# Ring loads issued first, the scaled input transposed a second time, and S5's kernel in one bank

## The chip, the cores and the metric

One core of a Trainium2 chip runs the whole program in one launch. The metric is the device time in microseconds (us) of one execution; the median of several is given. The engines are TensorE (PE in the rows; PEld is its weight load), VectorE (DVE), ScalarE (ACT), GpSimd (POOL) and SyncE (SP); each works through its own instructions in order and waits on semaphores for the others. SP issues the weight loads, ACT and POOL issue a few DMAs as well.

## What is computed

The reference is three layers over a sequence of 256 tokens with 1024 features, each with a modulation of its normed input by a condition vector. What matters here is the first step of the first layer and one constant matrix of the third:

```python
def ada_modulate(x, c, norm_g, ada_w, ada_b):
    ada = jax.nn.silu(c) @ ada_w + ada_b
    shift, scale, gate = jnp.split(ada, 3, axis=-1)
    h = rmsnorm(x, norm_g) * (1.0 + scale[:, None, :]) + shift[:, None, :]
    return h, gate[:, None, :]

def s5_mixer(u, lambda_re, lambda_im, log_dt, b_re, b_im, c_re, c_im, d_skip, glu_w, glu_b):
    ...
    lam_bar = jnp.exp(lam * dt)
    b_bar = ((lam_bar - 1) / lam)[..., None] * b
    bu = jnp.einsum('gpc,bsgc->bsgp', b_bar, uf.astype(jnp.complex64))
    _, states = lax.associative_scan(_ssm_combine, (a, bu), axis=1)
    y = jnp.einsum('gcp,bsgp->bsgc', c, states).real \
        + d_skip.astype(jnp.float32).reshape(SSM_GROUPS, SSM_GROUP_CH) * uf
```

## The kernel before, in words

**Weights and products.** All weights are f32 in HBM and stream through `ring`, ten slots of 128x1024 (512 KB each), loaded by SP in the order of `unit_list`. A unit is two slots ("halves"). A slot of a product's weights is rounded by ACT to fp32r (`WH`, in `cut` at L1088, four buffers), DVE subtracts to get the rest (`WL`, L1530, four buffers), and PE makes three matmuls per tile: high times high, high times low, low times high (`mm3`, all recorded at L554). A slot of modulation weights ("ada", 16 halves for the first two thirds, shift and scale, of the first layer) is not multiplied on PE as a rule: DVE adds slot times silu(c) into `ACC` (chunk 0, shift) or `ACC2` (chunk 1, scale, in `SQT`), L1543 for a chunk's first half and L1546 for the others; PE then sums over the partitions with `ones` (`ada_sum`, 8 matmuls). The halves in `ADA_PE` go to PE instead (`ada_half`). An f32 matmul leaves two records in the trace, an fp32r one or a transpose one.

**The start.** The ten ring slots begin to be loaded behind nine small loads of vectors (`packs[0]`) on SP. PE transposes the vectors (`vc0`), x as it is (`xt0` to `xt3`, 16 transposes, copied to `xT` by ACT), does halves 1 and 3 by `ada_half`, spreads the rsqrt of the mean squares over the partitions (`r0`), does `vc1`, half 6, the sum of chunk 0, half 11, half 14 and the sum of chunk 1, with `warm` matmuls (of the identity, their result unused) in between. DVE makes the other halves, then the low parts of two weight slots (`cut(1 - AHEAD_L)`), then both additions of the bias, `GS` = (1 + scale) times gain, and `modulate`: for each of eight blocks of 128 features, SQT = xT * GS * r (L1626), then ACT rounds SQT + shift to `hh`, then DVE makes `hl` (L1631). The first product, `v0`, is 48 matmuls of 256 columns and begins when block 0 is there. `M0` holds the modulation's result, `SIL` the silu(c).

**S5's kernel.** In the third layer the matrices `TOEP` are made beside the first feed-forward (`ffn`), by generators that advance one step for each half unit (`side.run`). `s5_weights` makes 16 products of `BK` (128 x 32) with `CL` (128 x 128), real and imaginary part added up, so 32 f32 matmuls: four groups `tp0` to `tp3` of eight, each in a bank of its own taken from the rotation (`open_`), partitions 0 to 31, with one step between them. ACT copies each group into four diagonal blocks of TOEP, four copies per group and one group per step. DVE adds `ssm_d` to the diagonal afterwards (`s5_skip`). There are four rotating PSUM banks, `pw`; a bank opened with `hold` comes back into the rotation by `back` only.

## Time and profile before

| | us |
|---|---|
| median of 3 runs | 1041.58 |
| lowest, highest | 1039.48, 1042.46 |
| the profiled execution, device time | 1039.8 |
| its span in the trace | 1038.1 |
| TensorE busy | 999.2 (96%) |
| VectorE busy | 720.7 (69%) |
| ScalarE busy | 507.7 (49%) |
| mean granted TensorE clock | 0.995 of full |

The profiled execution is 1.8 us below the median. Its device time is 1.7 us more than its span. TensorE is busy nearly throughout, so that a microsecond counts where TensorE waits, runs at a lower clock, or has fewer instructions to do. The DMA engines are busy 95% or more over most of the first 50 us and 40 to 75% afterwards.

### The profile page before, as it was taken

What the parts mean: (1) busy time and instruction counts of PE and PEld (TensorE: products, weight loads), DVE (VectorE), ACT (ScalarE), POOL (GpSimd) and SP (SyncE); (2) the same over time, 40 slices, a digit from 0 to 9 for tenths busy, and PEclk for the clock granted to TensorE, in tenths of its full rate; (3) what the DMA queues carried; (4) which work ended last, traced back from release to release, by engine and by line L of the source; (5) the groups of instructions that cost most, each with busy time, mean ns of one, the idle gap of its engine ahead of it and who ended that gap; (6) DMA issues with size and microseconds to landing.
All of it is one profiled execution on the core that took longest, in us unless ns stands there. A gap on an engine that the chain in (4) does not pass through costs nothing.

```text
span 1038.1 us, 19534 instructions
## 1 busy us (share of the span) xinstructions
PE 999.2 (96%) x8198; PEld 987.0 (95%) x8198; DVE 720.7 (69%) x1021; ACT 507.7 (49%) x741; POOL 41.0 (4%) x67
## 2 busy tenths in 40 slices
PE   6999999999999999999999999999997999999998
PEld 5899999999999999999999999998997999999998
DVE  4767876777746845667999788678877666465554
ACT  2554354456544454634754564555465454444442
POOL 2100000000000013401000000000000000000000
PEclk9999999999999999999999999999998999999999
DMA  9987486656764976469477667664433446466621
GB/s 355 366 279 244 163 284 244 218 189 229 258 203 134 315 242 214 155 245 298 152 247 263 233 244 247 240 236 153 160 103 105 139 154 208 166 227 195 212 98 42
DMA packets 138960, 219.58 MB, mean 212 GB/s; under 512 B 7161, under 2 KB 110922, under 8 KB 138872
## 3 DMA queue, kind: packets, MB, share of 16 engines
q1 hardware_dynamic: 136776, 214.00, 59.9%
q10 hardware_dynamic: 1136, 2.58, 0.7%
q0 software_dynamic: 960, 1.76, 0.6%
q8 instruction: 65, 1.06, 0.4%
q14 instruction: 23, 0.19, 0.1%
HBM read 217.25 MB, written 1.05 MB: 210 GB/s over the span
## 4 chain that ended last, share of the span: by engine, by line
PE 86%; DVE 7%; issue 2%; ACT 2%; DMA 2%; SPq 0%; ACTq 0%; DVEq 0%
PE pw L554 63%; PE pacc L554 22%; DVE WL L1530 2%; DMA ring<-in_even_in_w 1%; ACT AR L1088 1%; DVE hl L1631 1%; DVE SQT L1626 1%; DVE ACC L1546 1%; DMA AR<-in_cond 0%; ACT hh L1088 0%; ACT WH L1088 0%; PE pw L935 0%; PE pw L722 0%; SPq L311 0%; ACT YH L1088 0%
## 5 line engine op out<-in xcount | busy, mean ns | idle before, releaser
L1088 ACT ACTIVATE WH<-ring 128x1024 fp32r<-128x1024 f32 x288 | 302.0, 1055 | 268.8 <-PE pw L554 190.8
L554 PE MATMUL pw<-hh,WH 128*128 128x256 f32 x1408 | 404.2, 287 | 8.3 <-DVE WL L1530 4.3
L1530 DVE TENSOR_TENSOR WL<-ring,WH 128x1024 fp32r<-128x1024 f32 x288 | 344.3, 1223 | 81.5 <-ACT WH L1088 81.0
L554 PE MATMUL pw<-hl,WH 128*128 128x256 f32 x1408 | 399.0, 283 | 0.0
L554 PE MATMUL pw<-hh,WL 128*128 128x256 f32 x1408 | 399.0, 283 | 0.0
L554 PEld LDWEIGHTS pw<-hh,WH 128*128 128x128 f32 x1408 | 270.4, 192 | 12.1 <-issue 9.9
L554 PEld LDWEIGHTS pw<-hl,WH 128*128 128x128 f32 x1408 | 270.5, 192 | 0.0
L554 PEld LDWEIGHTS pw<-hh,WL 128*128 128x128 f32 x1408 | 270.4, 192 | 0.0
L554 PE MATMUL pacc<-YH,WH 128*128 128x256 f32 x672 | 192.6, 287 | 3.5 <-issue 2.5
L554 PE MATMUL pacc<-YH,WL 128*128 128x256 f32 x672 | 191.0, 284 | 0.0
L554 PE MATMUL pacc<-YL,WH 128*128 128x256 f32 x672 | 191.0, 284 | 0.0
L1088 ACT ACTIVATE AR<-pw 128x512 f32<-128x512 f32 (+5 forms) x196 | 86.2, 453 | 129.4 <-PE pw L554 128.5
L554 PEld LDWEIGHTS pacc<-YH,WH 128*128 128x128 f32 x672 | 129.6, 193 | 4.4 <-issue 4.4
L554 PEld LDWEIGHTS pacc<-YL,WH 128*128 128x128 f32 x672 | 129.7, 193 | 0.0
L554 PEld LDWEIGHTS pacc<-YH,WL 128*128 128x128 f32 x672 | 129.7, 193 | 0.0
L1546 DVE SCALAR_TENSOR_TENSOR ACC<-ring,PC,ACC 128x1024 f32<-128x1024 f32 x95 | 122.0, 1284 | 7.7 <-DMA ring<-in_ada_w 2.0
L554 PE MATMUL pw<-WH,hh 128*128 128x256 f32 x192 | 55.4, 289 | 2.3 <-DVE hl L1631 2.2
L2035 DVE TENSOR_TENSOR AR<-AR,pw 128x256 f32<-128x256 f32 x44 | 16.5, 418 | 58.9 <-ACT AR L1088 58.9
L1575 DVE TENSOR_TENSOR YL<-AR,YH 128x512 fp32r<-128x512 f32 x48 | 32.8, 691 | 34.7 <-ACT YH L1088 34.5
L554 PE MATMUL pw<-AR 128*128 128x128 f32 (+6 forms) x416 | 55.9, 287 | 0.9 <-ACT AR L1088 0.9
L554 PE MATMUL pw<-WH,hl 128*128 128x256 f32 x192 | 55.2, 287 | 0.0
L554 PE MATMUL pw<-WL,hh 128*128 128x256 f32 x192 | 55.1, 287 | 0.0
(245 smaller groups left out, 853.4 us busy)
## 6 DMA issues: line engine op xcount, KB each, us to landing
ring<-in_w_mod SPq DMA_DIRECT2D x72, 512.0 KB, 5.8
ring<-in_odd_in_w SPq DMA_DIRECT2D x56, 512.0 KB, 6.9
ring<-in_ada_w SPq DMA_DIRECT2D x48, 512.0 KB, 8.0
ring<-in_ffn_w_gate SPq DMA_DIRECT2D x44, 512.0 KB, 5.0
ring<-in_ffn_w_up SPq DMA_DIRECT2D x44, 512.0 KB, 5.3
ring<-in_ffn_w_down SPq DMA_DIRECT2D x44, 512.0 KB, 4.8
ring<-in_even_in_w SPq DMA_DIRECT2D x40, 512.0 KB, 6.8
ring<-in_even_out_w SPq DMA_DIRECT2D x16, 512.0 KB, 5.8
```

What stands on the lines that cost most here:

```text
L554: return eng.matmul(o, a, b, start=start, stop=stop, skip_group_check=True)
L1088: return eng.activation(dst, src, func, **kw)
L1530: tt(WL[:, i % NL, :], slot(half_of(i)), WH[:, i % NH, :].bitcast(F32), SUB).then_inc(s_lo, 1)
L1546: stt(out=acc, in0=slot(g), scalar=wc, in1=acc, op0=MUL, op1=ADD).then_inc(s_ada, 1)
L1575: tt(f2(YL[:, i % 3]), src, f2(YH[:, i % 3]).bitcast(F32), SUB).then_inc(s_yl, 1)
L1626: stt(out=SQT[:, k, :], in0=xT[:, k, :], scalar=GS[:, k:k + 1], in1=rb, op0=MUL, op1=MUL).then_inc(s_u, 1)
L1631: stt(out=hl[:, q, :], in0=SQT[:, q, :], scalar=m[:, q:q + 1], in1=hh[:, q, :].bitcast(F32), op0=ADD, op1=SUB).then_inc(s_hl, 1)
L2035: tt(fbuf(blk, m), fbuf(blk, m), pw[b][:, T:2 * T], MUL).then_inc(s_bank[b], 1)
```

## The change

- **Queues at the start.** SP issues nothing but ring loads. `packs[0]` now holds only `c` and `cond` and goes first on ACT's queue, then the identity, then x; the other seven vectors (`packs[1]`) and the rest of `consts` are issued by ACT after the two Exp. POOL has the last two packs, and its later loads wait for ring load 19 where they waited for 15.
- **Order of the modulation.** The scale half of the weights is loaded first (chunk 0 is now the scale, chunk 1 the shift). PE takes halves 1, 3, 6, 9 and 12.
- **x times r.** ACT multiplies XN by the rsqrt (two passes of 128x1024 into `XR`), PE transposes that too (`xr0` to `xr3`, 16 transposes), ACT copies it to SQT and multiplies it by GS. The spread `r0` and the L1626 pass of DVE are gone for the first layer. The shift is summed and added in two halves (`ada1a`, `ada1`), and hh and hl of blocks 0 to 3 follow the first. One weight slot is cut ahead of them where three (ACT) and two (DVE) were.
- **S5's kernel.** One bank `tp`, held: the matmul of index m writes partitions 32m to 32m+31, index q the columns. 32 matmuls in one step, m innermost, seven steps later the bank returns. ACT's 16 copies stay four to a step.

```diff
-ADA_PE = (1, 3, 6, 11, 14)
+ADA_PE = (1, 3, 6, 9, 12)
...
-    units += ada(a0, 0, 2)
+    units += ada(a0, 1, 2) + ada(a0, 0, 1)
...
-    for key, ms in (("p0", (0, 2, 4)), ("p1", (5, 7, 8, 9, 10)), ("p2", (12, 13)), ("p3", (15,))):
+    for key, ms in (("p0", (0, 2, 4)), ("p1", (5, 7)), ("p2", (8, 10)), ("p3", (11,)), ("p4", (13, 14, 15))):
...
             p.wait_ge(d_vec[0], n_vec[0])
             pb = open_("vc0")
             close(eng.transpose(pb[:, 0:n0], VR[0:n0, 0, :], ident[0:n0, 0:n0]), "vc0")
...
             ada_half(1)
             ada_half(3)
+            p.wait_ge(d_x, 16)
+            turn(XN, "xt")
...
+            close(last, "vc1")
+            ada_half(6)
+            p.wait_ge(s_xr, 2)
+            turn(XR, "xr")
+            p.wait_ge(*ada_done(7))
...
-            close(eng.transpose(pb[:, n1:n1 + n2], VR[0:n2, 2, :], ident[0:n2, 0:n2]), "vc1")
-            ada_half(6)
-            ada_sum(0)
-            ada_half(11)
+            ada_sum(0, range(8), "ada0")
...
+            p.wait_ge(*gone["ada0"])
+            ada_half(9)
+            ada_half(12)
+            warm(8, "warm0a")
+            p.wait_ge(*ada_done(15))
+            ada_sum(1, range(4), "ada1a")
+            ada_sum(1, range(4, 8), "ada1")
+            warm(8, "warm0c")
...
                 for q in range(4):
-                    pb = open_(f"tp{q}")
-                    for m in range(4):
-                        for i in range(2):
-                            last = mm(pb[0:32, m * P:m * P + P], BK[i][:, 4 * q + m, :], CL[i][:, 4 * q + m, 0:P],
-                                      m == 0 and i == 0, i == 1)
-                    close(last, f"tp{q}")
-                    yield
+                    for i in range(2):
+                        for m in range(4):
+                            last = mm(pb[32 * m:32 * m + 32, q * P:q * P + P], BK[i][:, 4 * q + m, :],
+                                      CL[i][:, 4 * q + m, 0:P], q == 0 and i == 0, i == 1)
+                close(last, "tp")
+                yield from idle(7)
+                back("tp")
...
+            s.wait_ge(s_r, 1)
+            for m in range(2):
+                act(XR[:, m, :], XN[:, m, :], scale=RS[:, m:m + 1]).then_inc(s_xr, 1)
+            for q in range(4):
+                evac(f"xr{q}", SQT[:, 2 * q:2 * q + 2, :], src=v3(pw[place[f"xr{q}"]][:, :], 2))
             evac("dt", DTC, src=pw[place["dt"]][:, 0:16], func=ACT.Exp)
+            s.wait_ge(s_gs, 1)
+            for k in range(8):
+                s.wait_ge(*gone[f"xr{k // 2}"])
+                act(SQT[:, k, :], SQT[:, k, :], scale=GS[:, k:k + 1]).then_inc(s_u, 1)
...
-            pack_loads(eng.dma_start, 1, d_vec[1])
             pack_loads(eng.dma_start, 2, d_vec[2])
...
-            g.wait_ge(*landed(15))
+            g.wait_ge(*landed(19))
```

How the order of the engines moves, at three places. TensorE, from the first layer's last modulation halves to the first product (`pacc<-PC,ring` is `ada_half`, `pacc<-cst,ACC` or `SQT` or `AR` a sum of a chunk, `pw<-cst` a warm, `pw<-WH,hh` the first product's first matmul); the kernel before:

```order
L554 MATMUL pacc<-PC,ring 128x128 [waits s_ring1]
L554 MATMUL pacc<-PC,ring 128x128 x7
L740 MATMUL pw0<-cst,AR 128x16 [waits s_lam,s_bank0]
L554 MATMUL pw1<-cst 128x128 [waits s_fill]
L554 MATMUL pw1<-cst 128x128 x7
L554 MATMUL pacc<-PC,ring 128x128 [waits s_ring4]
L554 MATMUL pacc<-PC,ring 128x128 x7
L554 MATMUL pw3<-cst 128x128 [waits s_bank3]
L554 MATMUL pw3<-cst 128x128 x3
L554 MATMUL pacc<-cst,SQT 128x128 [waits s_ada]
L554 MATMUL pacc<-cst,SQT 128x128 x7
```

and the changed one, from its sum of the scale chunk on:

```order
L557 MATMUL pacc<-cst,ACC 128x128 [waits d_cst,s_ada]
L557 MATMUL pacc<-cst,ACC 128x128 x7
L750 MATMUL pw2<-cst,AR 128x16 [waits s_lam,s_bank2]
L557 MATMUL pacc<-PC,ring 128x128 [waits s_ring9,s_mod]
L557 MATMUL pacc<-PC,ring 128x128 x7
L557 MATMUL pacc<-PC,ring 128x128 [waits s_ring2]
L557 MATMUL pacc<-PC,ring 128x128 x7
L557 MATMUL pw3<-cst 128x128 [waits s_bank3]
L557 MATMUL pw3<-cst 128x128 x7
L557 MATMUL pacc<-cst,AR 128x128 [waits s_ada]
L557 MATMUL pacc<-cst,AR 128x128 x7
```

Halves 9 and 12 now stand behind the addition of the scale (`s_mod`), and nothing but one warm stands between them and the last sum.

VectorE, from the last modulation half to the first hl; the kernel before:

```order
L1546 SCALAR_TENSOR_TENSOR SQT<-ring,PC,SQT 128x1024 [waits s_ada,s_ring5]
L1530 TENSOR_TENSOR WL<-ring,WH 128x1024 [waits s_hi] x2
L1551 TENSOR_TENSOR MOD<-pacc,VC 128x8 [waits s_fill]
L1551 TENSOR_TENSOR MOD<-pacc,VC 128x8
L1615 SCALAR_TENSOR_TENSOR PC<-MOD,VC 128x8 [waits s_mod]
L1626 SCALAR_TENSOR_TENSOR SQT<-xT,PC,pw2 128x256 [waits s_v]
L1626 SCALAR_TENSOR_TENSOR SQT<-xT,PC,pw2 128x256
L1631 SCALAR_TENSOR_TENSOR hl<-SQT,MOD,hh 128x256 [waits s_hh]
```

and the changed one, from half 10 on:

```order
L1574 SCALAR_TENSOR_TENSOR AR<-ring,PC,AR 128x1024 [waits s_ada,s_ring0]
L1672 TENSOR_TENSOR MOD<-pacc,VC 128x8 [waits s_fill,s_bank1]
L1704 SCALAR_TENSOR_TENSOR PC<-MOD,VC 128x8 [waits s_mod]
L1574 SCALAR_TENSOR_TENSOR AR<-ring,PC,AR 128x1024 [waits s_ada,s_ring1]
L1708 TENSOR_TENSOR RS<-VC,PC 128x16 [waits s_bank2]
L1574 SCALAR_TENSOR_TENSOR AR<-ring,PC,AR 128x1024 [waits s_ada,s_ring3]
L1574 SCALAR_TENSOR_TENSOR AR<-ring,PC,AR 128x1024 [waits s_ada,s_ring4]
L1574 SCALAR_TENSOR_TENSOR AR<-ring,PC,AR 128x1024 [waits s_ada,s_ring5]
L1672 TENSOR_TENSOR MOD<-pacc,VC 128x4 [waits s_fill]
L1558 TENSOR_TENSOR WL<-ring,WH 128x1024 [waits s_hi]
L1678 SCALAR_TENSOR_TENSOR hl<-SQT,MOD,hh 128x256 [waits s_hh,s_u,s_mod]
```

The scale's addition stands ahead of four halves; behind the last half one low part (L1558) is left where two were, and no L1626.

TensorE at the first group of S5's kernel (`32x128`), the kernel before and the changed one:

```order
L554 MATMUL pw2<-hh,WL 128x256
L554 MATMUL pw3<-AR 32x128 [waits s_bank3,s_cl,s_bk]
L554 MATMUL pw3<-AR 32x128 x7
L554 MATMUL pw0<-hh,WH 128x256 [waits s_lo]
L554 MATMUL pw0<-hl,WH 128x256
```

```order
L557 MATMUL pw0<-hh,WL 128x256
L557 MATMUL pw2<-AR 32x128 [waits s_bank2,s_cl,s_bk]
L557 MATMUL pw2<-AR 32x128 x31
L557 MATMUL pw3<-hh,WH 128x256 [waits s_lo]
L557 MATMUL pw3<-hl,WH 128x256
```

All 32 stand in one place, ahead of the last quarter of a feed-forward block.

## Rows read from the trace of the kernel before

**Rows 1.** The page's busy times: us, share of the span, instructions.
```profile
PE 999.2 (96%) x8198; PEld 987.0 (95%) x8198; DVE 720.7 (69%) x1021; ACT 507.7 (49%) x741; POOL 41.0 (4%) x67
```
**Rows 2.** What TensorE waited for, whole span: us in total, times, longest.
```profile
PE pw L716 <- DMA AR<-in_cond: 9.2, 1, 9.2
PE pw L554 <- DVE hl L1631: 5.0, 5, 2.2
```
**Rows 3.** The chain of waits, first 45 us: start us, us, what.
```profile
21.74 10.95 DMA ring<-in_even_in_w
...
33.80 1.23 DVE WL L1530
```
**Rows 4.** Timeline, 20 to 45 us: start, us, engine, line, what [idle before].
```profile
29.70 1.28 DVE L1546 SCALAR_TENSOR_TENSOR SQT<-ring,PC,SQT 128x1024 f32<-128x1024 f32 x1 [1.28 <-DMA ring<-in_ada_w]
...
31.11 1.97 PE L554 MATMUL pacc<-cst,SQT 128*128 128x128 f32 x16
31.21 1.06 ACT L1088 ACTIVATE WH<-ring 128x1024 fp32r<-128x1024 f32 x1 [2.54 <-DMA ring<-in_even_in_w]
...
34.21 1.06 ACT L1088 ACTIVATE WH<-ring 128x1024 fp32r<-128x1024 f32 x1 [0.45 <-DMA ring<-in_even_in_w]
34.94 0.23 DVE L1551 TENSOR_TENSOR MOD<-pacc,VC 128x8 f32<-128x8 f32 x2
...
36.47 0.49 DVE L1631 SCALAR_TENSOR_TENSOR hl<-SQT,MOD,hh 128x256 fp32r<-128x256 f32 x1 [0.18 <-ACT hh L1088]
...
37.10 0.36 PE L554 MATMUL pw<-WH,hh 128*128 128x256 f32 x1 [2.22 <-DVE hl L1631]
...
41.84 1.28 ACT L1157 ACT_TABLE_LOAD   x1
```
**Rows 5.** Stretches: us, busy (records) of each engine, PEclk, DMA share, GB/s.
```profile
0.00:9.00 9.00, 0.00 (x0) 0.00 (x0) 0.00 (x0) 1.28 (x1) 6.87 (x17) 1.00 0.76 254
4.00:9.00 5.00, 0.00 (x0) 0.00 (x0) 0.00 (x0) 0.00 (x0) 4.01 (x9) 1.00 1.04 361
9.00:25.00 16.00, 14.83 (x107) 14.46 (x108) 11.89 (x26) 4.32 (x10) 0.00 (x0) 1.00 1.03 410
37.00:42.00 5.00, 4.90 (x28) 4.93 (x29) 4.82 (x13) 3.21 (x7) 0.00 (x0) 0.66 1.06 350
```
**Rows 6.** Timeline, first 20 us: start, us, engine, line, what [idle before].
```profile
4.37 15.37 SPq L2295 DMA_DIRECT2D ring<-in_ada_w  x16
9.17 0.43 PE L716 MATMUL pw<-cst,AR 116*128 116x116 f32 x1 [9.17 <-DMA AR<-in_cond]
...
9.39 3.62 PE L722 MATMUL pw<-cst,AR 128*128 128x128 f32 x16
...
11.07 0.75 DVE L1543 TENSOR_SCALAR ACC<-ring,PC 128x1024 f32<-128x1024 f32 x1
...
12.81 4.42 PE L554 MATMUL pacc<-PC,ring 128*128 128x128 f32 x32
15.09 1.28 DVE L1546 SCALAR_TENSOR_TENSOR ACC<-ring,PC,ACC 128x1024 f32<-128x1024 f32 x1 [1.23 <-DMA ring<-in_ada_w]
```
**Rows 7.** Timeline, end of the program: its 16 output transposes.
```profile
1031.26 1.91 PE L1075 MATMUL pw<-cst,AR 128*128 128x128 f32 x16
```
**Rows 8.** Timeline around S5's groups `tp0` and `tp1`, ScalarE and TensorE.
```profile
669.77 1.78 ACT L1088 ACTIVATE AR<-pw 32x128 f32<-32x128 f32 x4 [0.87 <-PE pw L554]
...
672.46 0.28 PE L554 MATMUL pw<-hh,WL 128*128 128x256 f32 x1
672.67 1.93 PE L554 MATMUL pw<-AR 128*32 128x128 f32 x16
674.53 0.39 PE L554 MATMUL pacc<-YH,WH 128*128 128x256 f32 x1
674.76 0.28 PE L554 MATMUL pacc<-YL,WH 128*128 128x256 f32 x1
674.88 0.28 PE L554 MATMUL pacc<-YH,WL 128*128 128x256 f32 x1
```

More of the change, by code:

```diff
@@ L339, in build @@
         d_id, d_cst, d_x = sem("d_id"), sem("d_cst"), sem("d_x")
-        d_vec = [sem(f"d_vec{a}") for a in range(3)]
-        n_vec = [16 * len(packs[0]), 16 * len(packs[1]), 16 * (len(packs[2]) + 1)]
+        d_vec = [sem(f"d_vec{a}") for a in range(4)]
+        n_vec = [16 * len(pk) for pk in packs[:3]] + [16 * (len(packs[3]) + 1)]
         d_sguw, d_sgub, d_glr, d_glw = sem("d_sguw"), sem("d_sgub"), sem("d_glr"), sem("d_glw")
@@ L351, in build @@
         s_silu = sem("s_silu")
+        s_xr = sem("s_xr")
+        s_gs = sem("s_gs")
         s_x2 = sem("s_x2")
@@ L420, in build @@
         fg = col("final_g", 0, 8)
-        ACC2 = f2(SQT[:, 0:4, :])
+        ACC2 = ar(14720, 1024)
         GT = v3(ar(0, 4096), 16)
@@ L513, in ysc @@
             return last
-        full, gone, place = {}, {"ada0": (s_mod, 1), "ada1": (s_mod, 2)}, {}
+        full, gone, place = {}, {"ada0": (s_mod, 1), "ada1": (s_mod, 3)}, {}
         block = ctx.enter_context(nc.Block())
@@ L693, in norm_mod @@
                 back(f"r{L}")
-            n0, n1, n2 = pack_n
+            n0, n1, n2, n3 = pack_n
             def ada_half(m):
@@ L703, in ada_half, with ada_sum @@
                     last = mm(pacc[:, j, c * P:c * P + P], slot(g)[:, j * P:j * P + P],
-                              SIL[:, m % 8:m % 8 + 1].to_broadcast([P, P]), m in (1, 11) and j % 2 == 0, False)
+                              SIL[:, m % 8:m % 8 + 1].to_broadcast([P, P]), m == 1 and j % 2 == 0, False)
                 last.then_inc(s_adp, 1)
-            def ada_sum(c):
-                p.wait_ge(*ada_done(8 * c + 7))
-                for j in range(8):
+            def ada_sum(c, js, name):
+                for j in js:
                     last = mm(pacc[:, j, c * P:c * P + P], (ACC, ACC2)[c][:, j * P:j * P + P], ones, False, True)
-                close(last, f"ada{c}")
+                close(last, name)
             p.wait_ge(d_id, 16)
@@ L740, in _ @@
             close(eng.transpose(pb[:, 0:16], DTR, ident[0:16, 0:16]), "dt")
-            warm(8, "warm0b")
-            ada_half(14)
-            warm(4, "warm0c")
-            ada_sum(1)
-            warm(8, "warm0d")
-            back("r0")
+            p.wait_ge(*gone["ada0"])
[6 more added lines that the diff above has]
+            warm(8, "warm0c")
             for j in range(4):
@@ L1125, in yhigh, with modulate @@
                 act(f2(YH[:, i % 3]), src).then_inc(s_yh, 1)
-            def modulate(L, sh):
-                for k in range(8):
+            def modulate(L, sh, ks=range(8)):
+                for k in ks:
                     s.wait_ge(s_u, 8 * L + k + 1)
@@ L1387, in s5_prep @@
                 s.wait_ge(s_tz, 7)
-                for q in range(4):
-                    b = place[f"tp{q}"]
-                    pb = pw[b][:, :].rearrange("p (a t n) -> p a t n", a=4, t=4)
-                    s.wait_ge(*full[f"tp{q}"])
+                b = place["tp"]
+                pb = v3(pw[b][:, :], 4)
+                s.wait_ge(*full["tp"])
+                for m in range(4):
                     for blk in range(4):
-                        r = slice(32 * blk, 32 * blk + 32)
-                        to = TOEP[r, 4 * q:4 * q + 4, 32 * (3 - blk):].rearrange("p a (t n) -> p a t n", n=32)
-                        last = act(to, pb[0:32, :, 0:blk + 1, :])
-                        if blk < 3:
+                        last = act(TOEP[32 * blk:32 * blk + 32, m:16:4, 32 * (3 - blk):],
+                                   pb[32 * m:32 * m + 32, :, 0:32 * blk + 32])
+                        if m < 3 or blk < 3:
                             last.then_inc(s_tp, 1)
@@ L1548, in ada @@
                     elif what == "add":
[L1549 to L1553 removed]
+                        v.wait_ge(*full[f"ada{c}"])
                         b = place[f"ada{c}"]
@@ L1642, in update, with first_add, first_lows @@
                 v.wait_ge(s_x, X_FIN[L] + 8)
-            n0, n1, n2 = pack_n
+            def first_add(c, to, j0, n, name):
+                v.wait_ge(*full[name])
+                tt(MOD[:, to:to + n].unsqueeze(2), pacc[:, j0:j0 + n, c * P:c * P + 1],
+                   col("ada_b", to, n).unsqueeze(2), ADD).then_inc(s_mod, 1)
+            def first_lows(ks):
+                for k in ks:
+                    v.wait_ge(s_hh, k + 1)
+                    stt(out=hl[:, k, :], in0=SQT[:, k, :], scalar=M0[:, k:k + 1], in1=hh[:, k, :].bitcast(F32),
+                        op0=ADD, op1=SUB).then_inc(s_hl, 1)
+            n0, n1, n2, n3 = pack_n
             v.wait_ge(*full["vc0"])
@@ L2017, in s5_skip @@
                 yield from idle(6)
-                v.wait_ge(s_tp, 12)
-                for q in range(4):
-                    v.wait_ge(*gone[f"tp{q}"])
+                v.wait_ge(s_tp, 15)
+                v.wait_ge(*gone["tp"])
                 for b in range(4):
```

89 lines of the change are left out of this document (52 added, 37 removed).

## The prediction

> **What bounds the kernel now.** I read the busy times first: TensorE is busy 96% of the span [rows 1]. The list of what TensorE waited for comes next: 9.2 us at the very start, for `cond` to land, and 5.0 us in five waits for hl, of which the longest, 2.2, stands before the first product [rows 2]. From the first product on, at 37.10, TensorE has nearly no gap for 100 us. So the program is a start of 37.10 us and then TensorE's own work; a start that is earlier by a microsecond should end the program a microsecond earlier.
>
> What bounds the start? The chain of waits goes through DMA for 10.95 us from 21.74 [rows 3]. The timeline agrees: VectorE waited 1.23 us for modulation half 4 (used at 15.09) and 1.28 us for half 15 (used at 29.70) [rows 4, 6]. Eleven slots in 14.61 us are 1.33 us each, which is what 512 KB take at the 410 GB/s of that stretch [rows 5]. Behind half 15 stand VectorE's pass (1.28), the sum (31.11 to 33.1), but then no addition until 34.94: VectorE was still on a low part, 33.80 to 35.03 [rows 3, 4]. Addition, GS, SQT, hh and hl take the 2.1 us to 37.10. TensorE idled 2.2 us there, and over 37 to 42 its mean granted clock is 0.66 of full: it fell to the lower level, 1.2 GHz, after that pause [rows 4, 5].
>
> **DMA from the first moment.** In the first 9 us the queues moved 254 x 9 = 2.29 MB [rows 5]. The ring's first load was issued at 4.37 [rows 6]. If the ring is issued at 0.8 and data flows from about 2.3 us, 6.7 us at 361 to 410 GB/s are 2.42 to 2.75 MB: 0.3 to 1.1 us of loading ahead. I take 0.9, near the rate of the long stretch, because 4 KB rows of weights will then flow beside the small ones. Half 15 lands at 28.8, its pass ends at 30.1. The landing of c, cond and identity costs nothing: before, silu was ready at 11.07 [rows 6], and the first slot is not there before 7.5 or 8.
>
> **The scaled transposes.** They put a new chain on the start: half 4 (14.1), VectorE's pass and rsqrt (to 17.2), two ACT passes of 1.06 behind the copies of xt (to 20.4), 16 transposes, the sum of the scale, VectorE's addition, and only behind that halves 11 and 13 to 15. The transposes cost 1.9 us at full clock [rows 7] and 3.6 at the lower one [rows 6]; the trace shows that level for the first 16 and the higher one within the 32 records behind them. Where TensorE stands at each step: half 1 from 8.9 and half 3 from 12.8 (they wait for their slots), xt to 17.5, half 6 to 19.9, xr to 22.3, sum to 24.2. VectorE has finished half 10 at 23.2, waits 1.1 us for the sum, does the addition, GS and half 11 to 26.0, and half 13 lands at 26.1. So the new wait is just covered, with next to nothing to spare; every microsecond that it is later shows. Queued behind that addition on TensorE is half 9, and behind half 9's slot all of SP's later loads (piece 3 of the first product and on). Half 9 ends at 26.6, while the load before stands in the queue until 33: covered.
>
> **From half 15 to the first product.** Half 9 and 12 and a warm fill TensorE to 30.5. Half a sum is 1.0 us (half of 1.97, rows 4): the first half-addition is at 31.8. ACT's WH0 is made by then (31.21 + 1.06 less 0.9). hh0 to 32.4, low part 0 on VectorE 31.9 to 33.1, hl0 to 33.65. TensorE has the other half sum and a warm (2.0) until 34.4, so it begins at 34.4: **2.7 us earlier**, and without a pause. A mean of 0.66 over 5 us is 3.4 us at half the clock; 256 columns take 0.213 us at 1.2 GHz and 0.12 per record otherwise [rows 8], so 16 records took 0.093 longer each: **1.5 us** to gain if the clock holds. Against it: ACT has cut one slot ahead instead of three. It does hh0 to hh3, WH1, hh4 to hh7 (to 37.1), the table load of 1.28 [rows 4], then WH2 (to 39.5); low part 2 is ready at 40.7, and TensorE, 48 x 0.12 = 5.8 us after 34.4, wants it at 40.2: **0.5 lost**. The start gives 2.7 + 1.5 - 0.5 = 3.7. The piece that was last to be late there is WH3 (its slot is free once half 9 is done), wanted 3 us later.
>
> POOL's loads (1.1 MB for the spatial gate) now wait for ring load 19, 5 us later; the transposes that use them stand behind four products, 23 us after the start: nothing. SP loses nine issues. DVE loses eight passes and ACT gains fourteen (XR, the copies of xr, the multiplication by GS), the last of them between the scale's addition at 24.5 and WH0 at 30.2, 5.7 us for eight passes of about 0.5 (as hl, rows 4): covered.
>
> **S5's kernel.** A group of eight costs TensorE, from the matmul before (672.46) to the first after (674.53), 2.07, less the 0.12 that a matmul takes anyway, plus 0.11 by which the one after is longer (674.76 - 674.53 against 0.12): 2.06 us, 1.86 for 16 records and 0.2 for going in and out [rows 8]. Four groups: 8.2 us, all on the path, for TensorE has no gap there. In one group the 0.2 is paid once: 0.6 saved for sure. What 32 matmuls cost whose outputs lie in four different strips of partitions no row shows. They may run one after the other (0.6 saved), or four at a time: 64 x 0.116 / 4 = 1.9 + 0.2, 6.2 saved. I take two at a time, 3.7 + 0.2 = 3.9, **4.3 saved**, the middle: that the array's columns are free for it speaks for four, that every record of this trace, of 64, 128 or 256 columns, takes 0.11 to 0.12 us speaks for a cost per instruction that overlap doesn't remove. ACT's copies stay as they were (1.78 per step); the first waits for all 32, up to 675.4 instead of 669.8, while ACT has nothing due before the feed-forward's own copy, which stands behind TensorE's last 24 matmuls: covered. One bank less for seven steps leaves three; a block holds two, a modulation sum one, and a block's banks are copied out during the 5.8 us of the down projection: covered.
>
> The Trainium skill (TensorE: Matmul & The Clock Gate, Part 3: Packing small matmuls) has outputs in different 32-partition strips run concurrently, three of them measured 2.38 times as fast; by that the 7.4 us would be 3.1 and the sum 0.6 us better. No row here shows it.
>
> **Sum.** 3.7 + 4.3 = 8.0. The profiled execution of 1039.8 becomes 1031.8. It lies 1.8 below the median; what is compared are medians, so 1041.58 - 8.0 = **1033.6**.
>
> **Rivals.**
> 1. *The strips don't overlap.* 3.7 + 0.6 = 4.3, **1037.3**. For it: 0.11 to 0.12 us per record everywhere. Against: only 128-column weights were ever loaded at that rate.
> 2. *They overlap fully.* 3.7 + 6.2 = 9.9, **1031.7**.
> 3. *TensorE is at the lower clock during the second transposes.* The first 16 ran at 3.6 us, and the clock rose only within the halves behind them [rows 6]. Now TensorE's first 10 us are broken by waits for slots and followed by 32 transposes. If xr and the sum run at 1.2 GHz, they cost 1.6 + 1.5 more, with no cover: the start gives 0.6, in all 4.9 with the strips overlapped by two (**1036.7**), 1.2 without (1040.4). Against: the output transposes ran at full clock, but straight behind matmuls [rows 7]. The Trainium skill (TensorE: Matmul & The Clock Gate, Part 4: PE-mode transpose) says that transposes don't count as TensorE activity for the clock; rows 6 fit that and fit a plain delay as well.
> 4. *The ring overtakes what the start needs; slower.* Ring, c, cond, identity and x are now issued at the same moment. If c and cond were served behind the ten slots, 5.2 MB at 410 GB/s, they would land at 15 instead of 9. VectorE's eleven halves, rsqrt and copies are 15.6 us of work from there: half 15 done at 32.9, the scale chain adds 1, TensorE begins at 38.2. That is 1.1 later, with pause and clock as before, plus the 0.5 for low part 2, less 0.6 if the strips don't overlap: **1042.6**. It decides from a landing at about 14 us on. Against: `cond` landed 5.05 us after issue amid the same traffic.
>
> **Chances.** Forecast 0.38, rival 2 0.10, rival 1 0.26, rival 3 0.22, rival 4 0.04. The range of eight in ten goes from rival 2 less a microsecond of scatter, 1030.5, to rival 3's middle, 1039.5. A measurement of this kernel can tell about 0.3%, 3.1 us, from nothing. Faster by more: forecast and rival 2, most of rival 1 (4.3) and half of 3: 0.78. Within: 0.18. Slower: 0.04.
>
> **What would show it.** First product's first matmul at 34 to 35 us, with the clock at 1.00 in the 5 us behind it; VectorE idle about 1 us before the scale's addition; a wait of TensorE for WL of about 0.5 us near 40; one block of 64 records with `128*32` weights, about 3.7 us long (7.4 and 1.9 are rivals 1 and 2). A first matmul after 36, or xr at 3.4 us, is rival 3; silu after 14 is rival 4. I would be wrong altogether if the time won at the start were given back at a later wait; behind the first product DMA has slack (the share of its engines' time falls, see the table), so I don't expect that.

## The result, and the profile after

| | before | after |
|---|---|---|
| median, us (4 runs each, taken together) | 1041.21 | 1033.49 |
| lowest, highest | 1039.48, 1042.46 | 1031.64, 1034.32 |
| the profiled execution, device time | 1039.8 | 1033.03 |
| its span in the trace | 1038.1 | 1031.0 |
| TensorE busy | 999.2 | 992.2 |
| mean granted TensorE clock in it | 0.995 | 0.993 |

The ratio is 0.9925, 95% interval 0.9904 to 0.9945: 7.7 us less, where 8.0 were forecast. The sum came out; two of its terms did not, and their errors cancel, which is luck.

I read the timeline of the start first. TensorE of the changed kernel (start, length, engine and line, shapes, count; in brackets the idle time before and what ended it; L557 is before's L554):

```profile
7.43 0.28 PE L719 MATMUL pw<-cst,AR 16*128 16x16 f32 x1 [7.43 <-DMA cst<-in_consts]
9.09 5.30 PE L557 MATMUL pacc<-PC,ring 128*128 128x128 f32 x32 [1.38 <-DVE PC L1688]
14.23 1.91 PE L729 MATMUL pw<-cst,AR 128*128 128x128 f32 x16
...
19.05 1.97 PE L729 MATMUL pw<-cst,AR 128*128 128x128 f32 x16 [0.55 <-ACT AR L1101]
20.85 1.95 PE L557 MATMUL pacc<-cst,ACC 128*128 128x128 f32 x16
...
30.74 2.05 PE L557 MATMUL pacc<-cst,AR 128*128 128x128 f32 x16 [1.98 <-DVE AR L1574]
32.62 1.95 PE L557 MATMUL pw<-cst 128*128 128x128 f32 x16
34.33 0.36 PE L557 MATMUL pw<-WH,hh 128*128 128x256 f32 x1
...
40.40 0.36 PE L557 MATMUL pw<-WH,hh 128*128 128x256 f32 x1
```

Against [rows 4, 6]: both sets of 16 transposes take 1.9 us, where the first set took 3.62; the first product begins at 34.33 instead of 37.10; the second product's first matmul is at 40.40, 6.07 us behind it. VectorE over the same stretch:

```profile
21.51 1.28 DVE L1574 SCALAR_TENSOR_TENSOR AR<-ring,PC,AR 128x1024 f32<-128x1024 f32 x1 [1.22 <-DMA ring<-in_ada_w]
22.91 0.17 DVE L1672 TENSOR_TENSOR MOD<-pacc,VC 128x8 f32<-128x8 f32 x1
...
26.62 4.06 DVE L1574 SCALAR_TENSOR_TENSOR AR<-ring,PC,AR 128x1024 f32<-128x1024 f32 x3 [2.06 <-DMA ring<-in_ada_w]
31.93 0.16 DVE L1672 TENSOR_TENSOR MOD<-pacc,VC 128x4 f32<-128x4 f32 x1 [1.25 <-PE pacc L557]
32.01 1.21 DVE L1558 TENSOR_TENSOR WL<-ring,WH 128x1024 fp32r<-128x1024 f32 x1
33.14 1.66 DVE L1678 SCALAR_TENSOR_TENSOR hl<-SQT,MOD,hh 128x256 fp32r<-128x256 f32 x4
```

VectorE never waits for the scale's sum; it waits for slots, 1.2 and 2.1 us. Half 13 is there at 26.62. Then S5's kernel, TensorE's block with the matmul around it, and VectorE behind it:

```profile
664.75 0.28 PE L557 MATMUL pw<-hh,WL 128*128 128x256 f32 x1
664.96 1.96 PE L557 MATMUL pw<-AR 128*32 128x128 f32 x64
666.84 0.39 PE L557 MATMUL pw<-hh,WH 128*128 128x256 f32 x1
...
676.57 0.36 PE L557 MATMUL pw<-hh,WH 128*128 128x256 f32 x1 [0.82 <-DVE WL L1558]
```
```profile
670.50 0.75 DVE L2081 TENSOR_TENSOR AR<-AR,pw 128x256 f32<-128x256 f32 x2 [5.92 <-ACT AR L1101]
672.01 0.69 DVE L1599 TENSOR_TENSOR YL<-AR,YH 128x512 fp32r<-128x512 f32 x1 [0.76 <-ACT YH L1101]
672.62 2.66 DVE L1574 SCALAR_TENSOR_TENSOR ACC<-ring,PC,ACC 128x1024 f32<-128x1024 f32 x2
675.20 4.85 DVE L1558 TENSOR_TENSOR WL<-ring,WH 128x1024 fp32r<-128x1024 f32 x4
```

All 64 records in the time that 16 took [rows 8], and a new wait of 0.82 us for a low part ten microseconds later. Last, the clock, in stretches (PE, PEld, DVE, ACT and POOL busy, then PEclk, the granted clock; DMA share, GB/s), the changed kernel:

```profile
0.00:9.00 9.00, 0.28 (x1) 0.18 (x1) 0.81 (x5) 1.59 (x3) 6.87 (x17) 1.00 0.80 299
...
30.00:36.00 6.00, 5.26 (x46) 5.26 (x47) 4.75 (x10) 4.80 (x9) 0.50 (x1) 1.00 1.07 372
36.00:42.00 6.00, 5.93 (x50) 5.75 (x49) 4.59 (x8) 5.97 (x8) 2.35 (x4) 1.00 1.09 360
135.00:140.00 5.00, 3.23 (x21) 3.05 (x21) 4.90 (x6) 3.56 (x7) 0.00 (x0) 0.85 0.52 152
140.00:145.00 5.00, 5.00 (x36) 5.00 (x36) 2.38 (x3) 2.62 (x5) 0.00 (x0) 0.81 0.99 326
...
780.00:785.00 5.00, 3.64 (x18) 3.45 (x18) 4.41 (x13) 1.67 (x3) 0.00 (x0) 0.52 0.55 179
785.00:790.00 5.00, 3.48 (x22) 3.29 (x21) 1.96 (x8) 1.93 (x5) 0.00 (x0) 0.80 0.36 111
790.00:795.00 5.00, 4.01 (x23) 4.04 (x24) 4.62 (x9) 3.16 (x7) 0.00 (x0) 0.66 0.01 3
```

and the kernel before at the same pause of TensorE (1.8 us, at 140 there, at 136 after), with no fall:

```profile
140.00:145.00 5.00, 3.20 (x25) 2.83 (x24) 4.90 (x7) 3.37 (x7) 0.00 (x0) 1.00 0.67 204
```

The 1.00 of the first stretch says little: [rows 5] have it over 9 to 25 us too, though the 16 transposes at 9.39 took 3.62 us [rows 6], about twice the 1.91 of [rows 7]. The fall behind the first product's start is gone, one at 138 us has come, and the stretch around 780 to 795 is slower. Where the time went is seen best by landmarks. For every ScalarE record that two traces share in order, I took the difference of their starts, and the median of these around a point. Negative is earlier than the changed kernel, whose own times stand at the head:

| near (us, after) | 60 to 139 | 145 to 400 | 645 | 688 to 775 | 800 to the end |
|---|---|---|---|---|---|
| before | 3.96 | 2.76 | 2.78 | 7.87 | 7.08 |
| start_only | 0.34 | 0.56 | 2.05 | 7.13 | 4.96 |
| tp_only | 4.03 | 4.03 | 5.69 | 5.70 | 3.5 |
| tp_in_turn | 0.35 | -0.86 | -0.84 | 3.16 | 1.42 |
| tp_pairs | 0.12 | 0.14 | 1.85 | 3.19 | 2.34 |
| pe14 | 0.06 | 0.26 | 1.76 | 1.76 | 0.28 |
| ring_behind | 1.76 | 0.56 | 0.78 | 0.78 | -0.68 |
| tp_shift | 1.64 | 0.46 | 0.51 | 2.32 | 1.48 |
| fill_pause | 0.28 | -0.92 | -0.52 | -0.52 | -2.23 |
| no_warm0c | 0.35 | -0.86 | -0.10 | -0.10 | -2.28 |
| table_later | 0.11 | -1.10 | -0.32 | -0.31 | -1.80 |
| best | 0.21 | -1.00 | 0.53 | 0.53 | -2.08 |

Before minus after: 4.0 gained at the start (2.77 by the earlier first product, about 1.6 by the clock behind it, less the wait of 0.35 at 40), 1.2 lost at 138 us, 5.1 gained at S5's kernel (2.78 to 7.87), 0.8 lost around 780. Steps of 1.2 to 1.5 at 138 and 640, and of up to 2.2 around 780 to 800, come and go between kernels that are equal there. They go with falls of the clock, and the last experiments are about these. Steps of 0.2 to 0.9 between 400 and 500 us (ring_first, fill_pause, no_warm0c, table_later) have no fall beside them; their cause stays open.

### The profile page after: what moved, and what is told of

Its sections match the earlier page's. It is cut to its first block, busy times and chain, and to the rows that moved or that the text cites. A ratio compares the mean times of both kernels' runs of the same rounds, so it can differ in the third digit from the quotient of the medians.

```text
span 1031.0 us, 19531 instructions
## 1 busy us (share of the span) xinstructions
PE 992.2 (96%) x8191; PEld 980.8 (95%) x8191; DVE 717.1 (70%) x1014; ACT 514.4 (50%) x755; POOL 41.0 (4%) x67
## 3 DMA queue, kind: packets, MB, share of 16 engines
q0 software_dynamic: 960, 1.76, 0.6%
## 4 chain that ended last, share of the span: by engine, by line
PE 85%; DVE 8%; issue 3%; ACT 2%; DMA 2%; ACTq 0%; DVEq 0%
PE pw L557 63%; PE pacc L557 22%; DVE WL L1558 2%; DMA ring<-in_ada_w 1%; ACT AR L1101 1%; DVE ACC L1574 1%; DVE hl L1655 1%; DVE SQT L1650 1%; DMA cst<-in_consts 1%; DVE AR L1574 0%; ACT hh L1101 0%; PE pw L947 0%; ACT YH L1101 0%; DVE AR L2081 0%; ACT WH L1101 0%
## 5 line engine op out<-in xcount | busy, mean ns | idle before, releaser
L557 PE MATMUL pw<-hh,WH 128*128 128x256 f32 x1408 | 403.3, 286 | 9.1 <-DVE WL L1558 5.1
L1558 DVE TENSOR_TENSOR WL<-ring,WH 128x1024 fp32r<-128x1024 f32 x288 | 343.9, 1222 | 79.7 <-ACT WH L1101 76.4
L557 PE MATMUL pw<-hh,WL 128*128 128x256 f32 x1408 | 398.3, 283 | 0.0
L557 PE MATMUL pw<-hl,WH 128*128 128x256 f32 x1408 | 398.3, 283 | 0.0
L557 PEld LDWEIGHTS pw<-hh,WH 128*128 128x128 f32 x1408 | 269.9, 192 | 12.8 <-issue 10.7
L557 PEld LDWEIGHTS pw<-hl,WH 128*128 128x128 f32 x1408 | 270.0, 192 | 0.0
L557 PEld LDWEIGHTS pw<-hh,WL 128*128 128x128 f32 x1408 | 269.9, 192 | 0.0
L557 PE MATMUL pacc<-YH,WH 128*128 128x256 f32 x672 | 192.1, 286 | 3.5 <-issue 2.5
L557 PE MATMUL pacc<-YH,WL 128*128 128x256 f32 x672 | 190.6, 284 | 0.0
L557 PE MATMUL pacc<-YL,WH 128*128 128x256 f32 x672 | 190.6, 284 | 0.0
L557 PEld LDWEIGHTS pacc<-YH,WH 128*128 128x128 f32 x672 | 129.6, 193 | 4.0 <-issue 4.0
L557 PEld LDWEIGHTS pacc<-YL,WH 128*128 128x128 f32 x672 | 129.6, 193 | 0.0
L557 PEld LDWEIGHTS pacc<-YH,WL 128*128 128x128 f32 x672 | 129.4, 193 | 0.0
L557 PE MATMUL pw<-WH,hh 128*128 128x256 f32 x192 | 54.7, 285 | 0.2
L557 PE MATMUL pw<-WL,hh 128*128 128x256 f32 x192 | 54.3, 283 | 0.0
L557 PE MATMUL pw<-WH,hl 128*128 128x256 f32 x192 | 54.3, 283 | 0.0
L557 PE MATMUL pw<-AR 128*128 128x128 f32 (+6 forms) x416 | 50.1, 287 | 0.9 <-ACT AR L1101 0.9
```

Of the source, the lines that this page charges most:

```text
L557: return eng.matmul(o, a, b, start=start, stop=stop, skip_group_check=True)
L1558: tt(WL[:, i % NL, :], slot(half_of(i)), WH[:, i % NH, :].bitcast(F32), SUB).then_inc(s_lo, 1)
```

## The experiments

**One part alone.** `start_only` is the changed kernel with S5's kernel in four banks as before; `tp_only` is the kernel before with the new block.

> The changed kernel with S5's kernel as before (four groups in four banks). If the parts add up, the start alone gives what the changed kernel's trace shows at its second product, 4.0 us, less what the clock takes back. The changed trace has a fall of the clock at 138 us, behind a pause of TensorE of 1.8 us that the kernel before has as well (at 140) without a fall. Theory P (the fall depends on where the pause lies in time, and the start moves it there): the same fall here at 138, 1.2 us lost, first matmul of the S5 groups 2.8 us earlier than before (667.74), in all 2.8 us better than before, about 1038.4 if before is 1041.2. Rival Q (the change's data traffic or bank order behind the start causes it): no fixed place, other falls. Rival R (the start's gain survives in full): 4.0 better, 1037.2, no fall at 138. The new wait of 0.8 us for WL behind the S5 block (676.6 in the changed trace) is absent.

> The kernel before with S5's kernel in one bank, nothing else. The block of 64 records lasts 1.96 us as in the changed kernel; the path is 6.2 us shorter at its end, of which about 1.1 goes back by a wait for WL that comes some 9 us later, since TensorE comes sooner than VectorE can: net 5.1, about 1036.1 if before is 1041.2. If that wait were an effect of the start instead, net would be 6.2 (1035.0). No fall of the clock near 140 (as before), one at 38 us.

Measured, in 12 and 6 runs: start_only 1037.71, ratio 0.9962 (0.9947 to 0.9976), 3.5 us less than before's 1041.22; tp_only 1036.41, ratio 0.9944 (0.9923 to 0.9965), 4.8 less. Together 8.3, and both at once 7.7: within their intervals the parts add up. In tp_only TensorE waited 0.8 us once for WL between 660 and 702 us, in start_only and before never: the new wait belongs to the S5 block, not to the start. Theory P got no support, though: tp_only has the start of before, with the same pause at the same time (140.4), and its clock fell behind it, at 143 us, where I expected no fall. So the place of the pause in time doesn't decide it.

**How the strips overlap.** `tp_in_turn` finishes one strip before the next; `tp_pairs` alternates between two strips.

```diff
-                for q in range(4):
-                    for i in range(2):
-                        for m in range(4):
+                for m in range(4):
+                    for q in range(4):
+                        for i in range(2):
```
```diff
-                for q in range(4):
-                    for i in range(2):
-                        for m in range(4):
+                for m0 in (0, 2):
+                    for q in range(4):
+                        for i in range(2):
+                            for m in (m0, m0 + 1):
```

> The changed kernel with the same 32 matmuls into the same bank and strips, but all eight of a strip before the next strip (m is the outer loop). If it is the overlap of neighbours in different strips that makes the block 1.96 us long, it is now about 64 x 0.116 = 7.4 us plus 0.2. If it were the single entry and exit, or a lower cost of these matmuls in a strip layout as such, it stays near 2.

> The changed kernel with the 32 matmuls of S5's kernel ordered so that only strips 0 and 1 alternate in the first 16 and strips 2 and 3 in the last 16 (the changed kernel goes round all four strips; a run with one strip after the other took 5.96 us for the 64 records, the changed one 1.96). If what counts is how many different strips are under way at once, this takes about twice 1.96, 3.5 to 4.1 us. If overlap comes from neighbouring instructions that merely differ in strip, it takes 2.0 to 2.4.

The block in tp_in_turn and, below it, in tp_pairs (timeline of TensorE, with the wait that follows):

```profile
664.12 5.96 PE L557 MATMUL pw<-AR 128*32 128x128 f32 x64
679.73 0.36 PE L557 MATMUL pw<-hh,WH 128*128 128x256 f32 x1 [0.82 <-DVE WL L1558]
```
```profile
666.81 3.29 PE L557 MATMUL pw<-AR 128*32 128x128 f32 x64
679.75 0.36 PE L557 MATMUL pw<-hh,WH 128*128 128x256 f32 x1 [0.83 <-DVE WL L1559]
```

5.96, 3.29 and 1.96 us for one, two and four strips under way: 1.8 and 3.0 times as fast. It is the round over the strips that makes the overlap, not the single bank; 3.29 is a little under the 3.5 to 4.1 that I expected by the number of strips, and well above the 2.0 to 2.4 of the other reading. The Trainium skill (TensorE: Matmul & The Clock Gate, Part 3: Packing small matmuls) gives 2.38 for three strips, measured with 512 columns; with 128 columns no run here has three, and 2.38 lies between the two and the four strips above. My 7.6 us for the one strip was too much: 0.093 us a record, not 0.116.

The two runs answer a second question. The 0.82 us wait is the same in all three though the block is 0, 1.3 and 4.0 us longer. So it is not that VectorE fell behind a TensorE that had saved more. Behind the block ScalarE copies out the down projection (670.08 in the changed kernel, 673.25 and 673.26 in the other two), and from there VectorE needs two additions, YL, two modulation halves and one WL, so that TensorE starts 6.48 to 6.49 us after that copy in all three. Before, TensorE did another group of eight (1.93 us) in this stretch [rows 8]; pulling the groups together took that cover away. Net savings by the landmarks (645 to 688 us) are 1.09, 3.75 and 5.09 us in turn, in pairs and in fours; gross ones (8.24, four groups of 2.06, less the block and its 0.13 of going in and out) are 2.15, 4.82 and 6.15. So 1.06 to 1.07 us is given back each time, 0.82 of it in that wait.

**The block elsewhere.** `tp_shift` moves it three steps back (idle 22, 18 and 9 for 19, 15 and 6 on TensorE, ScalarE and VectorE).

> The changed kernel with the whole S5 block three steps later on TensorE, ACT and VectorE, so that it stands half a feed-forward block away. Theory: of the 6.2 us that the block saves TensorE, 0.8 to 1.1 are given back at 676 to 688 us, where VectorE, which stood still until 670.5 for the down projection's result, has two modulation halves and then the low parts to make; three steps later VectorE has no such pause behind the block and TensorE waits less there: landmarks at 700 us 0.5 to 1 earlier than in the changed kernel against the same point before the block. Rival: VectorE and ACT set the pace in this stretch wherever the block stands (they are 6 us behind once TensorE is 6 us faster), and the same 0.8 to 1.1 us are lost within the next 30 us.

The theory's expectation fell, and so did the rival's size. The wait near 677 went, but a larger one came (timeline of TensorE, tp_shift):

```profile
695.76 0.36 PE L557 MATMUL pacc<-YH,WH 128*128 128x256 f32 x1 [2.23 <-DVE WL L1558]
```

The landmarks stand at +0.5 before the block and +2.3 behind it: 1.8 us less saved than in the changed kernel. So moving the block did not bring back what the wait costs; at the new place VectorE was further behind.

**DMA at the start.** `ring_first` is the kernel before with its nine small loads on ACT's queue, so that the ring goes out at once; `ring_behind` is the changed kernel with seven of these loads ahead of the ring on SP.

```diff
+            pack_loads(eng.dma_start, 0, d_vec[0])
             eng.dma_start(cst[:, 0:P], I["consts"][:, 0:P]).then_inc(d_id, 16)
...
-            pack_loads(eng.dma_start, 0, d_vec[0])
             piece_at = {half_of(n): n for n in range(NPIECE)}
```

> The kernel before with its nine small vector loads issued by ScalarE ahead of the identity and x, so that SP begins with the ring loads at 0.8 us instead of 4.4. Theory D (the start was bound by loading, and loading ahead is worth what the first 9 us carry more): half 15 lands 0.3 to 1.1 us earlier, first product at 36.0 to 36.8 instead of 37.10. Rival S (x, now issued at 4.5 us and behind ring loads, comes late): x lands after 13 us, TensorE does its transposes before halves 1 and 3 and all slots come free later; first product at 37.5 to 39, slower by 0.5 to 2.

> The changed kernel with the seven other vectors' loads issued by SP ahead of the ring again, as in the kernel before, instead of by ACT behind the Exp; so the ring's first load is issued about 3 us later, all else as changed. It tells what the early issue of the ring alone is worth. Theory: little, since in the changed kernel half 13 landed only 0.4 us before its time in the kernel before (26.6 against 27.05) though the ring was issued 3.5 us earlier: half 13 lands at 26.9 to 27.2, the first product at 34.6 to 34.9. Rival: the queue's lead is worth its full time and something else (x, c, identity in the same queues) ate it: half 13 lands at 28 or later and the first product at 35.7 or later.

ring_first: 1041.36, ratio 1.0003 (0.9986 to 1.0019). The time equals before's, but not for lack of an effect. Its first TensorE rows:

```profile
10.98 0.46 PE L716 MATMUL pw<-cst,AR 116*128 116x116 f32 x1 [10.98 <-DMA cst<-in_consts]
15.95 1.33 PE L722 MATMUL pw<-cst,AR 128*128 128x128 f32 x5 [4.51 <-DMA AR<-in_x]
```

TensorE's first transpose came 1.8 us later than in [rows 6], those of x began at 15.95 instead of 9.39, and the first product at 39.84, 2.7 later, which is later even than rival S's 37.5 to 39; the landmarks of 60 to 120 us stand at +5.96, 2.0 later than before. What made up for it was the clock, by the means over its runs and before's: none of its 12 runs was below 0.993 and nine were at 0.997 or 0.998, where before's lie at 0.989 to 0.996. So the early ring alone, with the order of the other loads as it was, is a loss at the start. That is rival 4's mechanism, and c and cond alone ahead of identity and x avoid it: the identity lands at 7.4, x at 12.4.

ring_behind: the ring's first load at 3.44 instead of 0.81, half 13 used at 28.38 instead of 26.62, first product at 36.09 instead of 34.33 (landmarks +1.76). My theory (0.4) was wrong and the rival right: in the changed kernel's arrangement 2.63 us of lead are worth 1.76. The chain of the scale also lost its cover there; VectorE waited for its sum:

```profile
26.28 0.17 DVE L1671 TENSOR_TENSOR MOD<-pacc,VC 128x8 f32<-128x8 f32 x1 [1.58 <-PE pacc L557]
```

Half 13 was still waited for behind that (0.45 us), so that the first product follows the loads. The single run gave 1032.08, less than the changed kernel's median, because its clock fell less: not at 138 (step from +1.76 to +0.56), and less around 780 (from +0.78 to -0.68). One time of one run says nothing at this size, the landmarks do.

**What sets the first product now.** `pe14` gives half 12 to VectorE and half 14 to TensorE; `no_warm0c` leaves out the eight warm matmuls behind the last sum; `table_later` does that and moves ScalarE's table load behind the first four products' copies.

> The changed kernel, with modulation half 12 on VectorE and half 14 on TensorE (before its last sum, in place of two of the warm matmuls). Theory V (VectorE's own work behind the landing of half 13 sets the first product): in the changed kernel VectorE is idle for 1.2 and 2.1 us before half 13 lands at 26.6, then makes halves 13, 14 and 15 without a wait to 30.7, and sums, addition, hh and hl take 3.6 to the first product at 34.33. With half 12 in the idle 2.1 us and half 14 gone, VectorE ends at 13's landing + 2.6 = 29.3 or, if half 15 lands later than that, at its landing (26.6 + 2 x 1.3 = 29.2) + 1.35 = 30.6 less what the queue is ahead. First product at 33.0 to 33.8, whole program 0.5 to 1.3 us earlier than the changed kernel (1032.2 to 1033.0 in the median). Rival D (the last half's landing sets it, not VectorE): first product within 0.2 of 34.33. Rival C (less warm work, the clock falls before the first product): records of 0.21 behind it and 1.2 us or more lost.

> The changed kernel without the eight warm matmuls behind its last modulation sum. In the changed kernel they end at 34.3 us, while the first hl is there at about 33.6. Theory N (the first product is not what bounds the start any more; low part 2 is): the first product's first matmul moves from 34.33 to 33.6, but the second product still waits for the low part of slot 2, which VectorE has at 40.3, because ACT makes WH2 only behind eight hh, WH1 and the table load; its gap grows from 0.35 to about 1.0 us, and from 45 us on the kernel stands within 0.1 us of the changed one. Rival: the 0.7 us stay, and every landmark from 45 us on is 0.6 to 0.7 earlier. Rival 2: the pause of 0.8 us left by the warm matmuls brings the clock down to 1.2 GHz, and 1 to 1.5 us are lost.

> As the run without those warm matmuls, and ACT's load of the silu table (1.28 us at 36.64) behind the four copies of the first products instead of ahead of WH2. By theory N, WH2 and low part 2 come 1.28 us earlier (39.0 instead of 40.3), which is before TensorE wants them at 39.4, so the 0.7 us of the earlier first product stay, and the 0.35 us gap goes as well: landmarks from 45 to 130 us 0.6 to 1.0 us earlier than in the changed kernel. Rival: half 9's slot or another load behind it is next, and less than 0.3 is left.

pe14 (5 runs): 1032.43, ratio 0.9898 (0.9879 to 0.9916), against the changed kernel's 0.9925 (0.9904 to 0.9945): not to be told apart, and its landmarks to 139 us are at +0.06. Its first product began at 34.39, within the 0.2 of rival D; theory V fell. TensorE and VectorE of pe14:

```profile
28.18 2.05 PE L557 MATMUL pacc<-PC,ring 128*128 128x128 f32 x16 [1.45 <-DMA ring<-in_ada_w]
```
```profile
25.59 2.67 DVE L1574 SCALAR_TENSOR_TENSOR AR<-ring,PC,AR 128x1024 f32<-128x1024 f32 x2 [0.81 <-DMA ring<-in_ada_w]
29.46 1.28 DVE L1574 SCALAR_TENSOR_TENSOR AR<-ring,PC,AR 128x1024 f32<-128x1024 f32 x1 [1.20 <-DMA ring<-in_ada_w]
```

Both engines wait for slots, and half 15 is there at 29.46, with loads that ran 0.1 to 0.2 us later in this execution (half 10 at 21.72 against 21.51). In the changed kernel half 15 landed at 29.20 and VectorE comes to it at 29.3 (26.62 and two of 1.35): landing and VectorE's work are within 0.2 us of each other, so relief on one side shows nothing.

no_warm0c: VectorE's whole chain was 0.35 later there (WL at 32.36), by its DMA. The first product began at 34.12, so 0.56 earlier against that chain; the second product then waited 0.66 us for its low part:

```profile
34.12 0.36 PE L557 MATMUL pw<-WH,hh 128*128 128x256 f32 x1 [0.98 <-DVE hl L1677]
40.75 0.35 PE L557 MATMUL pw<-WH,hh 128*128 128x256 f32 x1 [0.66 <-DVE WL L1557]
```

and the landmarks stand at +0.34, the DMA's share: all of the 0.56 was given back, as theory N has it (its sizes were 0.7 and about 1.0). table_later: its chain was 0.57 later (WL at 32.58), no wait for a low part is left near 40, and the landmarks at 100 us stand at +0.11, so 0.46 us better against the chain, though the clock fell near 32 us in this execution; taken as it stands, the 0.6 to 1.0 that I expected didn't come. That the gap is gone fits the table load as what held low part 2; its full worth with a steady clock stays open.

**The clock.** `fill_pause` puts eight warm matmuls into the pause at 136 us; `best` has these, table_later's edits, and eight more each at 777 and 788 us:

```diff
+                        if g == 2:
+                            warm(8, "warmp")
                         p.wait_ge(s_yl, g + 1)
...
                 if half == 0:
+                    warm(8, "warmc")
                     pb = open_("cs")
...
             spread("cr", 0, 6)
+            warm(8, "warmd")
```

> The changed kernel with eight warm matmuls of the identity put before the wait on the low part of the pooled values at 136.4 us, where TensorE waits 1.8 us in both kernels. Theory: the fall to 1.2 GHz over 137 to 142 us in the changed kernel follows from this pause; with the pause filled the granted clock stays 1.00 in 130 to 150, the landmark behind it is 1.2 us earlier (first matmul of the third layer's first units 1.2 sooner), and the median is 0 to 1.2 us under the changed kernel's 1033.5, since not every run has the fall. Rival: the fall comes by its own schedule, whatever TensorE does there; then the clock falls in 130 to 150 all the same or at the next pause (near 640 or 780), and the sum of low-clock time in the program stays 10 us. Rival 2: the warm matmuls (8 x 0.23 = 1.9 us) end later than the wait does, and cost 0.1 to 0.5.

> All that has gained or should gain, in one: no warm matmuls ahead of the first product and the silu table later; eight warm matmuls in the pause at 136 us; eight more in the pauses of 1.9 us ahead of the conv branch's squares (779 us) and of 2.5 us ahead of the last output products (788.5 to 791.0). Expectation: 0.7 us at the start, 0.4 to 1.2 us at 138, and at 780 to 800 us up to 2.5 us, where the changed kernel spent 10.2 us at 1.2 GHz: median 1029.0 to 1031.5 against the changed kernel's 1033.5. If the clock's falls there don't hang on these pauses, or only move on to the next ones, the last part is 0 and the median 1031.5 to 1032.5. If the warm matmuls hold up work that was ready, landmarks at 785 or 792 us are 0.2 to 0.5 later.

fill_pause: 1032.15, ratio 0.991 (0.989 to 0.993). In its trace the clock holds over 130 to 150 us and the landmarks step by 1.2 there (+0.28 to -0.92), as the theory has it; the fall at 778 stayed. Its interval overlaps the changed kernel's. best: 1030.50 (1028.34 to 1032.09), ratio 0.9894 (0.9872 to 0.9916). The same stretches as above, in best:

```profile
30.00:36.00 6.00, 4.62 (x26) 4.36 (x27) 4.75 (x9) 4.38 (x8) 0.00 (x0) 0.72 1.07 371
...
135.00:140.00 5.00, 5.00 (x42) 4.72 (x40) 4.89 (x7) 3.78 (x7) 0.00 (x0) 1.00 0.54 169
...
634.00:640.00 6.00, 3.90 (x21) 3.88 (x21) 6.00 (x6) 1.06 (x1) 0.00 (x0) 0.72 0.89 286
...
780.00:785.00 5.00, 3.64 (x31) 3.45 (x30) 4.79 (x13) 1.67 (x3) 0.00 (x0) 1.00 0.49 139
785.00:790.00 5.00, 3.89 (x30) 3.31 (x28) 2.75 (x10) 2.70 (x6) 0.00 (x0) 1.00 0.49 170
790.00:795.00 5.00, 4.83 (x41) 4.86 (x42) 4.47 (x8) 3.45 (x7) 0.00 (x0) 1.00 0.11 11
```

With the pauses filled the clock is 1.00 from 775 to 800 us, while in each of the other thirteen traces a fall starts between 778 and 795 us. The landmarks gain 2.6 us there against the changed kernel (+0.53 to -2.08); with the pauses open, fill_pause gains 1.7 and no_warm0c 2.2, so most of a 2.6 can also come by itself. The six runs of best have mean clocks of 0.997 to 1.000, those of the changed kernel 0.991 to 0.995, and no run with these pauses open is above 0.998. That speaks for the pauses at 777 and 788 as the cause of the falls there. Of the 0.7 us at the start nothing is to be seen in best's trace (+0.21), in which the clock fell at 32. For the pause at 136 the evidence is thin: of twelve profiled kernels that leave it open, five show the fall (after, start_only, tp_only, pe14, tp_pairs) and seven do not, so that two without it prove little. best's median is 3.0 us under the changed kernel's, but the intervals of their ratios overlap, and they ran on different occasions: likely faster, but not shown.

## Why the prediction was right, step by step

- **First product at 34.4: right (34.33), by partly wrong steps.** The lead in bytes was as worked out: 299 GB/s over 9 us is 2.69 MB, 0.40 MB more than [rows 5], 1.0 us at 410 GB/s (0.9 forecast). By the landings in the two traces 1.26 us of it reached halves 10 to 12 (half 12 landed at 24.05 instead of 25.31), but only 0.43 half 13 (26.59, 27.02) and 0.47 half 15 (29.20, 29.67; 28.8 was forecast). The lead was lost between halves 12 and 13: 2.54 us for one slot of 0.52 MB, at 399 GB/s over 24 to 26 us, so an estimated 1.0 MB. The other half of it belongs to other loads, probably to those behind the halves, which were issued from 18.53 on instead of 21.32. The miss did no harm, since the eight warm matmuls ended at 34.3 while the first hl was there at about 33.6: they had 0.6 us to give.
- **The new chain of the scale: covered, by more than forecast.** xt, xr and the addition came at 14.2, 19.05 and 22.91 instead of 15.6, 20.4 and 24.3; the silu was ready 2 us sooner than before. VectorE waited for slots, not for the sum. The cover hangs on the early ring: in ring_behind VectorE waited 1.58 us for the sum.
- **Low part 2 late by 0.5: right in kind** (a gap of 0.35 at 40.40; 0.66 without the warm matmuls). The table load was a part of it, as table_later shows.
- **1.5 us for the clock at 37 to 42: it came in this trace, but not for the reason given, and it isn't a sure gain of the change.** The profile shows it (7.3 us from first to second product before, 6.07 with a gap of 0.35 after, so about 1.6). The forecast rests on TensorE starting "without a pause". The pause didn't go; it moved ahead of the last sum, 1.98 us long (the row at 30.74) where it was 2.22 ahead of the first product. In the executions of tp_shift, table_later and best it was 2.40, 2.31 and 2.45 us long, and there the clock fell behind it all the same; tp_shift's row:

```profile
31.04 2.33 PE L557 MATMUL pacc<-cst,AR 128*128 128x128 f32 x15 [2.40 <-DVE AR L1574]
```

The changed kernel's profile paid 1.2 at 138 besides. 45 runs of the kernel before, taken beside the experiments, have a mean clock of 0.9932, the changed kernel's four 0.993: in these four the term gave nothing. Over the 25 runs of all seven kernels that have the changed start and leave the later pauses open (the changed kernel's own among them; pe14 and ring_behind alter the start a little) the mean is 0.9944, which at 0.76 us for each 0.001 (below) would be an estimated 0.9 us. So the term should have been between 0 and 0.9; which, stays open.
- **S5's kernel 4.3: the mechanism right, the size too small.** The block is 1.96 us, rival 2's 1.9, so 6.15 gross. The row on which I leaned, 0.11 to 0.12 us a record for whatever shape, speaks of matmuls that all need the same columns, and doesn't bear on ones that need different ones. "ACT has nothing due ... covered" looked at the wrong engine: the chain through VectorE took 1.06 us back. Net 5.1.
- **Sum.** 3.7 + 4.3 = 8.0 was forecast. Without the clock the traces give 2.4 at the start (2.77 by the first product, less 0.35) and 5.1 at the block, 7.5; the medians differ by 7.7. So the start's term was 1.3 too large, 1.5 of it the clock, while its rest (2.7 - 0.5 = 2.2) was 0.2 too small, and the block's was 0.8 too small. That 8.0 lies so near to 7.7 is in part luck.
- **Rivals.** 1 fell (5.96 us even in turn). 2 holds for the block, not for the total. 3 fell: xr took 1.97 us at a clock of 1.00. The Trainium skill's rule that transposes don't count for the clock (TensorE: Matmul & The Clock Gate, Part 4: PE-mode transpose) is not contradicted by this, since matmuls (32 records ahead of xt, 16 ahead of xr) stood before them. 4's mechanism exists (ring_first), but c, cond and identity at the head of ACT's queue kept clear of it.
